# Gate columns as float32 products in four column groups of the array, added by a 0/1 product

## The chip, the cores and the metric

The kernel runs on one core of a Trainium2 chip. The metric is device time in microseconds (us), the median of three runs.

## What is computed

Two transformer blocks on one sequence of 512 tokens of width 1024, all in float32. Block one begins with a root-mean-square norm and one wide projection, whose columns are split into thirteen parts. Three of these parts are very narrow: 8 columns `a_f`, 4 columns `b_i` and 4 columns `b_f`. They are the gates that the change is about.

```python
h = _rms(x, norm_mix_g[l])
z = h @ w_in + b_in
(a_q, a_k, a_v, a_f, b_qk, b_v, b_i, b_f, b_o, c_q, c_f, c_i, c_g) = _split_cols(z)
ca = jnp.cumsum(jax.nn.log_sigmoid(a_f.astype(f32)), axis=1).transpose(0, 2, 1)
ob = _mlstm_chunkwise(_heads(qb, B_HEADS), _heads(kb, B_HEADS), _heads(b_v, B_HEADS),
                      b_i.astype(f32).transpose(0, 2, 1), b_f.astype(f32).transpose(0, 2, 1))
```

## The kernel before, in words

**Products.** A large product is made from three matmuls of type fp32r: each operand is split into a high part (rounded by ScalarE) and a low part (the rest, by VectorE), and high times high, low times high and high times low are added in one bank (lines 1031 to 1033; 1301 to 1305 for the first tile pair). The activations of block one are `act_hi` and `act_lo`, made from `xin` (x transposed, 8 slices of 128 rows by 512 tokens) times the gain `g_mix`; the factor per token, `rsx`, is multiplied in where a tile leaves its bank.

**Weights.** They come in chunks of up to 2048 columns per partition. SyncE loads chunk c into `w_raw[c % 2]` once chunk c - 2 is split; ScalarE makes `w_hi[c % 3]` (line 1574) and VectorE `w_lo[c % 3]` (line 1918). When a chunk is split follows from a plan: chunk c is due after the last tile that reads chunk c - 3, unless the order names it (`w_later`).

**Tiles.** A tile is 128 output channels by 512 tokens in one PSUM bank, `ring0` or `ring1` in turn, or a bank of its own. TensorE says `tile_done`; VectorE drains the tile, and with that frees the ring (`ring_free`). Plain float32 matmuls are used beside these for small steps: `x_rs` (line 1081, ones times the squares, 128x512) and `hg_win` (line 1118), which runs as pairs, one matmul into partitions 0 to 63 and one into 64 to 127.

**Order.** One list of stages, `order`, is written out by hand, and every engine walks through it, each doing its own part of a stage. So a stage's place in the list is its place in every engine's queue. Around the change the list reads:

```python
        stage("w_later", 4)
        stage("hg_begin")
        products(2)
        in_tile("gates", 0, "gates")
        products(1)
        stage("gate_ln")
        ...
        for b in range(NB):
            stage("cb_a", b)
            fill_slot()
```

`hg_begin` and `products(n)` (stages `hg_att`, lines 2103 to 2109) are VectorE work of the HGRN heads; `fill_slot` puts one more `products(1)` and, at every fourth slot, four `hg_win` into the list. `cb_a` (four stages, 12 matmuls each) begins the tiles of `c_i` and `b_v` with chunk `cb0`, and `cb` ends them with chunk `cb1`. The gates are chunk 2: 1024 columns, of which 16 hold weights, and 24 matmuls of 128x512 (8 slices times 3). VectorE drains them into `gz` (line 1962), ScalarE adds the bias and makes the logarithms (stage `gate_ln`).

Of the kernel before, what the change touches and what calls it, by code (L numbers as in the profile page):

```python
# [99 lines left out]
def two_blocks(nc, xt_d, w_in_d, b_in_d, w_gate_d, w_out_d, w_up_d, w_down_d, pos_d, w_in2_d, lam_d, w_uq_d, w_ukv_d,  # L100
               w_pd_d, w_pm_d, w_out2_d, g_fin_d, par_d, con_d, out_d):
    ctx = ExitStack()
    with ctx:
        base = 1152

        def sb(name, shape, dt, kib):

            return nc.alloc_sbuf_tensor_at(name, shape, dt, offset=base + int(round(kib * KIB)))

        def sem(name):  # L110
            return ctx.enter_context(nc.semaphore(name))
# [10 lines left out]
        x_in = [sem(f"x_in{k}") for k in range(KD)]  # L122
        w_in0 = sem("w_in0")

        zeros_ready = sem("zeros_ready")

        x_sq, x_sum, x_ss, x_rs, x_hi, x_lo, x_col, z_in = (
# [7 lines left out]
        hg_a, hg_a_used, hg_q, hg_att_s, hg_kdT_mm, hg_kdT_s = (  # L135
            sem(n) for n in ("hg_a", "hg_a_used", "hg_q", "hg_att_s", "hg_kdT_mm", "hg_kdT_s"))

        hg_kd, hg_cross_mm, hg_sc, hg_u_mm, hg_u_s, hg_scan, hg_rep_mm, hg_dm, hg_in_mm, hg_o_mm, hg_n, hg_done = (
            sem(n) for n in ("hg_kd", "hg_cross_mm", "hg_sc", "hg_u_mm", "hg_u_s", "hg_scan", "hg_rep_mm", "hg_dm", "hg_in_mm", "hg_o_mm", "hg_n", "hg_done"))

        nrm_sq, nrm_mm, nrm_rs, nrm_done, qk_done = (sem(n) for n in ("nrm_sq", "nrm_mm", "nrm_rs", "nrm_done", "qk_done"))

# [60 lines left out]
        kdE = [sb(f"kdE{i}", [P, 2, NC, LC], F32, M + 44 + 4 * i) for i in range(2)]  # L203
        Ab = [sb(f"Ab{i}", [P, 2, T], F32, M + (12, 16, 28, 32, 36, 40)[i]) for i in range(6)]
        kd = sb("kd", [P, 2, NC, LC], F32, M + 20)
        kdT = sb("kdT", [P, 2, NB, P], F32, M + 24)
        qT = sb("qT", [P, 4, T], F32, M + 28)
        kT = sb("kT", [P, 4, T], F32, M + 36)
# [92 lines left out]
        def cc(name, r=slice(0, P)):  # L301
            at, n = CCOL[name]
            return con[r, at:at + n]

        def pc(name, i=0, n=1, r=slice(0, P)):
            return par[r, PCOL[name][0] + i:PCOL[name][0] + i + n]
# [34 lines left out]
        def chunk(name, *areas):  # L341
            parts, at = [], 0
            for sources in areas:
                if not isinstance(sources, list):
                    sources = [sources]
                nk, n = sources[0].shape[1], sum(src.shape[2] for src in sources)
                parts.append((at, nk, n, sources))
                at += nk * n
            assert at <= SLOT
            chunk_of[name] = len(chunks)  # L350
            chunks.append((name, parts, at))
# [24 lines left out]
        def stage(*s):  # L376
            order.append(s)
# [3 lines left out]

        in_chunk("c_f", OFF_CF)
        in_chunk("c_q", OFF_CQ)
        chunk("gates", w_gate_d)
        for q in range(2):
            chunk(f"cb{q}", [k_in[:, 4 * q:4 * q + 4, at:at + 256] for at in (OFF_CI, OFF_BV)])
        for i in range(2):
# [7 lines left out]
        def in_tile(kind, i, of):  # L395
            if (kind, i) in tile_at:
                last_use[chunk_of[of]] = tile_at[kind, i]
            else:
                tile((kind, i), of)
            stage(kind, i)  # L400
# [55 lines left out]
        begin("c_q", 1, KD)  # L456
        for p in range(2):
            in_tile("c_f", p, "c_f")
        in_tile("c_q", 0, "c_q")
        for p in range(2):  # L460
            stage("z", "c_f", p)
# [5 lines left out]
        stage("w_later", 4)  # L467
        stage("hg_begin")
        products(2)
        in_tile("gates", 0, "gates")  # L470
        products(1)
        stage("gate_ln")
        windows = iter(range(LC - 1, -1, -1))
        slots = itertools.count()

        def fill_slot():
            n = next(slots)
            if n % 4 == 3:
                for _ in range(4):
                    stage("hg_win", next(windows))  # L480
            if n < 13:
                products(1)

        for b in range(NB):
            stage("cb_a", b)
            fill_slot()
        for b in range(NB):
            in_tile("cb", b, "cb1")
# [405 lines left out]
        def bank_free(name):  # L894

            return ring_free[tile_at[name] % 2]

        def drains(name):

            return tile_at[name] // 2 + 1  # L900
# [61 lines left out]
        @block.sync  # L962
        def _(sp):
            x_k = xt_d.rearrange("(k p) t -> p k t", p=P)

            def weights_in(c):
                name, parts, n = chunks[c]
                for at, nk, w, sources in parts:
                    dst = raw[c % 2][:, at:at + nk * w].rearrange("p (k n) -> p k n", k=nk)
                    col = 0  # L970
                    for src in sources:
                        sp.dma_start(dst[:, :, col:col + src.shape[2]], src).then_inc(raw_in[c % 2], 16)
                        col += src.shape[2]

            def columns(c, k0, k1):
                return raw[c][:].rearrange("p (k n) -> p k n", k=KD)[:, k0:k1, :], chunks[c][1][0][3][0][:, k0:k1, :]

            for k in range(KD):
                sp.dma_start(xin[:, k, :], x_k[:, k, :]).then_inc(x_in[k], 16)
                sp.dma_start(*columns(0, k, k + 1)).then_inc(w_in0 if k == 0 else x_in[k], 16)  # L980
            sp.dma_start(*columns(1, 0, KD // 2)).then_inc(raw_in[1], 16)
            sp.dma_start(*columns(1, KD // 2, KD)).then_inc(raw_in[0], 16)
            sp.dma_start(con[:, 0:2 * P + 1], con_d[:, 0:2 * P + 1]).then_inc(con_in, 16)
            sp.dma_start(par[:, KD:], par_d[:, KD:]).then_inc(par_in, 16)
            sp.wait_ge(raw_in[0], 16)
            for c, (name, parts, n) in enumerate(chunks):
                if c >= 2:
                    wait_split(sp, c - 2)
                    weights_in(c)
                if c == 3:  # L990
                    sp.dma_start(con[:, 2 * P + 1:], con_d[:, 2 * P + 1:]).then_inc(rest_in, 16)
                    for i, (at, w) in enumerate(((OFF_AV, 512), (OFF_BV, 256), (OFF_CI, 256))):
                        to = (0, 512, 768)[i]
                        sp.dma_start(bias_t[:, to:to + w], b_in_d[at:at + w].partition_broadcast(P)).then_inc(rest_in, 16)
                    sp.dma_start(lamv[:].rearrange("p a b -> p (a b)"), lam_d.partition_broadcast(P)).then_inc(rest_in, 16)
                if name == "wo_b1":

                    sp.wait_ge(tile_done, upto(("yb", 1)))
                    sp.wait_ge(yb_n, 1)
                    for i in range(2):  # L1000
                        sp.dma_start(xT[:, 4 * i:4 * i + 4, :], x_k[:, 4 * i:4 * i + 4, :]).then_inc(x_back_in[i], 16)
                if name == "gate3":

                    sp.dma_start(posI[:], pos_d.partition_broadcast(P)).then_inc(pos_in, 16)

            sp.wait_ge(tile_done, upto(("pm", KD - 1)))
            sp.dma_start(gfin[:], g_fin_d.partition_broadcast(P)).then_inc(gfin_in, 16)
            for b in range(NB):
                for half, made in enumerate((out_act, out_dve)):
                    at = slice(512 * half, 512 * half + 512)  # L1010
                    sp.wait_ge(made, b + 1)
                    sp.dma_start(out_d.rearrange("(b p) d -> p b d", p=P)[:, b, at], xo[:, b, at]).then_inc(out_done, 16)
            sp.wait_ge(out_done, 32 * NB)
# [3 lines left out]
        def _(pe):  # L1017
# [57 lines left out]
            for s in order:  # L1075
                kind = s[0]
                if kind == "x_rs":

                    pe.wait_ge(con_in, 16)
                    pe.wait_ge(x_sum, KD - 1)  # L1080
                    pe.matmul(bank[4][:], cc("ones"), xsq[:, 0, :], start=True, stop=True).then_inc(x_ss, 1)
                elif kind == "gates":
                    channels(s, kind, 0, act)
                elif kind in ("c_g", "b_o"):
                    channels(s, kind, P * s[1], act, begun=begun.get(s, 0))
                elif kind in ("b_qk", "a_q", "a_k"):
# [73 lines left out]
                elif kind == "hg_in":  # L1160
                    p = s[1]
                    pe.wait_ge(hg_dm, 4)
                    for b in range(NB):
                        for hh in range(2):
                            r = slice(64 * hh, 64 * hh + 64)
                            mm = pe.matmul(bank[2 * p + hh][r, b * P:b * P + P], ci[:, b, (2 * p + hh) * HD:(2 * p + hh + 1) * HD],
                                           Dm[2 * p + hh][:, b, :], start=(b == 0), stop=False)
                    mm.then_inc(hg_in_mm, 1)
                elif kind == "hg_o":
                    p = s[1]  # L1170
                    pe.wait_ge(hg_scan, p + 1)
# [380 lines left out]
        def _(act):  # L1552
# [23 lines left out]
            for s in order:  # L1576
# [50 lines left out]
                    act.wait_ge(bank_free(s), drains(s))  # L1627
                    A(bo[:, s[1], :], bo[:, s[1], :], ACT.Sigmoid, bias=pc("b_bo", s[1])).then_inc(z_in, 1)
                elif kind == "gates":
                    act.wait_ge(bank_free(s), drains(s))  # L1630
                    A(gz[:], gz[:], ACT.Identity, bias=pc("b_gate", r=slice(0, 96))).then_inc(z_in, 1)
                elif kind == "gate_ln":

                    act.wait_ge(z_in, z_at["gates", 0])
# [264 lines left out]
        def _(dve):  # L1899
# [21 lines left out]
            for s in order:  # L1921
# [30 lines left out]
                elif kind in ("c_f", "c_q"):  # L1952
# [3 lines left out]
                    dve.wait_ge(x_rs, 1)  # L1956
                    to = cf[:, p] if kind == "c_f" else cq[:, p, :, 0:LC]
                    TT(to, v3(at_ring(s)[:], LC), v3(rsx[:], LC), ALU.mult).then_inc(bank_free(s), 1)
                elif kind == "gates":

                    dve.wait_ge(tile_done, upto(s))
                    TT(gz[:], at_ring(s)[0:96, :], rsx[0:96, :], ALU.mult).then_inc(bank_free(s), 1)
                elif kind in ("b_qk", "c_g", "b_o", "a_q", "a_k"):

                    i = s[1]
# [124 lines left out]
                elif kind == "hg_att":  # L2090
                    j = s[1]
                    n = LC - 1 - j
                    if n >= 6:
                        dve.wait_ge(hg_a_used, n - 5)
                    if n == 2:
                        dve.wait_ge(tile_done, upto(("gates", 0)))
                    q64 = cq[:].rearrange("p h c t -> p (h c) t")
                    f64 = cf[:].rearrange("p h c t -> p (h c) t")
                    k64 = ck[:].rearrange("p h c t -> p (h c) t")
# [533 lines left out]
```

## Time and profile before

| | |
|---|---|
| median of 3 runs | 1093.14 us (1093.06 to 1093.54) |
| span of the profiled execution | 1091.2 us (first to last instruction) |
| median less that span | 1.9 us |
| TensorE busy | 1078.4 us |
| VectorE busy | 713.4 us |
| ScalarE busy | 421.6 us |
| DMA over the span | 95.94 MB |

For the profiled execution only its span is listed. Busy times of TensorE overlap and their ends are modelled, so how long a matmul keeps the array is read from the chain of work, where each piece runs to the start of the next.

### The profile page before, as it was taken

The page shows a single profiled execution, that of the slowest core. Times are in us where ns is not written, and L with a number is a line of the kernel's source. Part 1 is how long each engine was busy: PE and PEld are TensorE (multiplying, and loading weights), DVE is VectorE, ACT ScalarE, POOL GpSimd, SP SyncE. Part 2 cuts the span into 40 slices and gives each one's busy share as a digit, 9 for nine tenths or more (in the row PEclk, how much of TensorE's full clock was granted, in tenths as well). Part 3 has the DMA queues.
Part 4 walks back from the last instruction along what each step waited for, and adds up shares of the span by engine and source line. Part 5 has one row for each costly group of instructions (what it writes and reads, how often), then busy time and mean ns, then how long its engine had stood idle before and what let it go on. Part 6 is the DMA issues. An engine that isn't in the chain of part 4 may idle for free.

```text
span 1091.2 us, 13622 instructions
## 1 busy us (share of the span) xinstructions
PE 1078.4 (99%) x5409; PEld 868.7 (80%) x5411; DVE 713.4 (65%) x1142; ACT 421.6 (39%) x663; POOL 0.2 (0%) x4
## 2 busy tenths in 40 slices
PE   9999999999999999999999999999999999999997
PEld 6877877877878888888888888887776777888886
DVE  6897877868768887754488745654568446364431
ACT  6612555334352323222222234744357443323232
POOL 0000000000000000000000000000000000000000
PEclk9999999999999999999999999999999999999999
DMA  8432121131213223233422134333121222033302
GB/s 256 121 116 78 39 77 41 57 136 39 78 39 126 97 97 106 58 87 101 151 78 87 49 97 154 92 102 116 44 78 39 78 77 78 1 117 115 111 25 77
DMA packets 100240, 95.94 MB, mean 88 GB/s; under 512 B 5953, under 2 KB 91089, under 8 KB 100177
## 3 DMA queue, kind: packets, MB, share of 16 engines
q1 hardware_dynamic: 100000, 95.05, 27.2%
q8 instruction: 43, 0.70, 0.3%
q14 instruction: 21, 0.16, 0.0%
q10 hardware_dynamic: 176, 0.02, 0.0%
HBM read 92.95 MB, written 2.10 MB: 87 GB/s over the span
## 4 chain that ended last, share of the span: by engine, by line
PE 94%; DVE 3%; ACT 1%; issue 1%; DVEq 0%; ACTq 0%
PE ring L1031 23%; PE ring L1033 22%; PE ring L1032 22%; PE bank L1031 3%; PE bank L1033 3%; PE bank L1032 3%; PE bank L1486 1%; PE bank L1281 1%; PE bank L1253 1%; PE bank L1186 1%; PE bank L1266 1%; PE bank L1118 1%; PE bank L1510 1%; PE bank L1459 1%; PE ring L1349 1%
## 5 line engine op out<-in xcount | busy, mean ns | idle before, releaser
L1031 PE MATMUL ring<-act_hi,w_hi 128*128 128x512 f32 (+1 forms) x816 | 323.5, 396 | 0.9 <-DVE xT L2302 0.5
L1033 PE MATMUL ring<-act_hi,w_lo 128*128 128x512 f32 (+1 forms) x816 | 316.7, 388 | 0.0
L1032 PE MATMUL ring<-act_lo,w_hi 128*128 128x512 f32 (+1 forms) x816 | 316.4, 388 | 0.0
L1574 ACT ACTIVATE w_hi<-w_raw 128x2048 fp32r<-128x2048 f32 (+4 forms) x97 | 160.9, 1659 | 248.1 <-PE ring L1033 212.8
L1918 DVE TENSOR_TENSOR w_lo<-w_raw,w_hi 128x2048 fp32r<-128x2048 f32 (+5 forms) x102 | 191.4, 1879 | 4.0 <-ACT w_hi L1574 3.7
L1031 PEld LDWEIGHTS ring<-act_hi,w_hi 128*128 128x128 f32 x816 | 153.3, 188 | 37.4 <-issue 3.9
L1032 PEld LDWEIGHTS ring<-act_lo,w_hi 128*128 128x128 f32 x816 | 153.3, 188 | 31.8 <-issue 1.9
L1033 PEld LDWEIGHTS ring<-act_hi,w_lo 128*128 128x128 f32 x816 | 153.2, 188 | 31.7
L1033 PE MATMUL ring<-hidH,w_lo 128*128 128x512 f32 x176 | 68.5, 389 | 0.0
L1031 PE MATMUL ring<-hidH,w_hi 128*128 128x512 f32 x176 | 68.5, 389 | 0.0
L1032 PE MATMUL ring<-hidL,w_hi 128*128 128x512 f32 x176 | 68.5, 389 | 0.0
L2336 DVE TENSOR_TENSOR zp<-ring,rsn 128x512 f32<-128x512 f32 x44 | 30.3, 689 | 41.6 <-PE ring L1033 37.0
L1911 DVE CUSTOM_DVE_ANT_0 bank<-bank,maskb 128x128 f32<-128x128 f32 (+3 forms) x80 | 37.7, 513 | 28.4 <-PE bank L1513 13.7
L2361 DVE TENSOR_TENSOR xT<-xT,ring 128x512 f32<-128x512 f32 x16 | 11.0, 686 | 58.1 <-PE ring L1033 58.1
L1032 PEld LDWEIGHTS ring<-hidL,w_hi 128*128 128x128 f32 x176 | 33.0, 188 | 6.9
L1031 PEld LDWEIGHTS ring<-hidH,w_hi 128*128 128x128 f32 x176 | 33.0, 188 | 6.8
L1033 PEld LDWEIGHTS ring<-hidH,w_lo 128*128 128x128 f32 x176 | 33.0, 188 | 6.8
L1574 ACT ACTIVATE hidH<-hid 128x512 fp32r<-128x512 f32 x22 | 13.8, 625 | 60.3 <-DVE hid L2349 60.3
L1574 ACT ACTIVATE Pf<-bank,small 128x128 f32<-128x128 f32 (+3 forms) x32 | 16.6, 523 | 31.4 <-DVE small L1911 31.4
L1574 ACT ACTIVATE sqn<-ring 32x512 f32<-32x512 f32 x36 | 21.2, 589 | 12.6 <-PE ring L1033 12.2
L1031 PE MATMUL bank<-w_hi,mH 128*128 128x512 f32 x64 | 25.7, 402 | 0.0
L1031 PE MATMUL bank<-w_hi,act_hi 128*128 128x512 f32 x64 | 25.4, 397 | 0.0
(360 smaller groups left out, 1624.4 us busy)
## 6 DMA issues: line engine op xcount, KB each, us to landing
w_raw<-in_w_in SPq DMA_DIRECT2D x30, 1024.0 KB, 5.1
w_raw<-in_w_up SPq DMA_DIRECT2D x22, 1024.0 KB, 5.0
w_raw<-in_w_out SPq DMA_DIRECT2D x8, 1024.0 KB, 5.0
w_raw<-in_w_down SPq DMA_DIRECT2D x8, 768.0 KB, 4.6
w_raw<-in_w_down SPq DMA_DIRECT2D x8, 640.0 KB, 4.3
w_raw<-in_w_in SPq DMA_DIRECT2D x7, 512.0 KB, 5.8
xin<-in_xt SPq DMA_DIRECT2D x8, 256.0 KB, 4.2
xT<-in_xt SPq DMA_DIRECT2D x2, 1024.0 KB, 6.6
```

The costliest lines, as they stand in the source:

```text
L1031: pe.matmul(out, ah, bh, start=(first and n == 0), stop=False)
L1032: pe.matmul(out, ah, bl, start=False, stop=False)
L1033: mm = pe.matmul(out, al, bh, start=False, stop=(last and n == len(pairs) - 1))
L1118: mm = pe.matmul(v3(bank[0][64 * p:64 * p + 64, :], LC)[:, :, first:], con[:, row:row + 64], v3(Ab[n % 6][:, p, :], LC)[:, :, first:], sta ...
L1186: pe.matmul(nrm_bank(n)[:], cc("blk"), scr[n % 2][:], start=True, stop=True).then_inc(nrm_mm, 1)
L1253: pe.matmul(bank[e][:, 0:n], qT[r, h // 2, qb * P:qb * P + P], kT[r, h // 2, 0:n], start=True, stop=False)
L1266: mm = pe.transpose(bank[2 + u % 2][:, b * P:b * P + P], Pf[u % 4][:, b * P:b * P + P], ident)
L1574: return act.activation(out, src, func, **more)
L1911: return dve.tensor_tensor_reduce(scores[:, 0:n], scores[:, 0:n], maskb[:, T - n:T], -1.0, 3.0e38, ALU.add, ALU.min, least)
L1918: return TT(dst, full, hi.bitcast(F32), ALU.subtract)
L2336: TT(z[:, 2:T + 2], at_ring(s)[:], rsn[:], ALU.mult).then_inc(bank_free(s), 1)
L2361: TT(xT[:, j, :], xT[:, j, :], at_ring(s)[:], ALU.add).then_inc(bank_free(s), 1)
```

## The change

The gates no longer form a chunk of weights. A table `wg` of 352 columns is loaded near the start: 8 blocks of 32 columns (16 of them used), one for each slice of `xin`, and a 0/1 table of 96 columns. VectorE multiplies the 256 weight columns by `g_mix` (stage `gate_w`). Stage `gatep` makes 8 plain float32 matmuls of 32 columns by 512 tokens, straight from `xin`: in two rounds of four, each of the four into another 32 partitions of one bank. VectorE drains the bank times `rsx` into `scr1`. Stage `gates` is now one float32 matmul of the 0/1 table with `scr1`, which adds the four groups and puts the rows where the rest wants them; it stands behind the first `cb_a`. ScalarE adds the bias from the bank.

```diff
@@
+        wg = sb("wg", [P, KD * 32 + 96], F32, M + 24)
@@
         in_chunk("c_f", OFF_CF)
         in_chunk("c_q", OFF_CQ)
-        chunk("gates", w_gate_d)
@@
             in_tile("c_f", p, "c_f")
+        stage("gate_w")
         in_tile("c_q", 0, "c_q")
@@
         stage("hg_begin")
         products(2)
-        in_tile("gates", 0, "gates")
+        tile(("gatep", 0))
+        stage("gatep", 0)
         products(1)
-        stage("gate_ln")
@@
             stage("cb_a", b)
+            if b == 0:
+                stage("gates", 0)
+                stage("gate_ln")
             fill_slot()
@@ sync
             sp.dma_start(par[:, KD:], par_d[:, KD:]).then_inc(par_in, 16)
+            sp.dma_start(wg[:], w_gate_d).then_inc(gate_in, 16)
@@ tensor
+                elif kind == "gatep":
+                    out = open_bank(s)
+                    pe.wait_ge(gate_w, 1)
+                    for r in range(2):
+                        for j in range(4):
+                            at = 32 * (2 * j + r)
+                            mm = pe.matmul(out[32 * j:32 * j + 32, :], wg[:, at:at + 32], xin[:, 2 * j + r, :], start=(r == 0), stop=(r == 1))
+                    mm.then_inc(tile_done, 1)
                 elif kind == "gates":
-                    channels(s, kind, 0, act)
+                    pe.wait_ge(bank_free(("gatep", 0)), drains(("gatep", 0)))
+                    pe.matmul(bank[4][0:96, :], wg[:, KD * 32:], scr[1][:], start=True, stop=True).then_inc(x_ss, 1)
@@ scalar
                 elif kind == "gates":
-                    act.wait_ge(bank_free(s), drains(s))
-                    A(gz[:], gz[:], ACT.Identity, bias=pc("b_gate", r=slice(0, 96))).then_inc(z_in, 1)
+                    act.wait_ge(x_ss, 2)
+                    A(gz[:], bank[4][0:96, :], ACT.Identity, bias=pc("b_gate", r=slice(0, 96))).then_inc(z_in, 1)
@@ vector
-                elif kind == "gates":
+                elif kind == "gate_w":
+                    dve.wait_ge(gate_in, 16)
+                    by_k = wg[:, 0:KD * 32].rearrange("p (k n) -> p k n", k=KD)
+                    TT(by_k, by_k, wide(pc("g_mix", 0, KD), 32), ALU.mult).then_inc(gate_w, 1)
+                elif kind == "gatep":
 
                     dve.wait_ge(tile_done, upto(s))
-                    TT(gz[:], at_ring(s)[0:96, :], rsx[0:96, :], ALU.mult).then_inc(bank_free(s), 1)
+                    TT(scr[1][:], at_ring(s)[:], rsx[:], ALU.mult).then_inc(bank_free(s), 1)
@@
                     n = LC - 1 - j
                     if n >= 6:
                         dve.wait_ge(hg_a_used, n - 5)
-                    if n == 2:
-                        dve.wait_ge(tile_done, upto(("gates", 0)))
```

As chunk 2 is gone, every later chunk has a number less by one: `cb0` is now chunk 2 and is split in its place early in the program (2048 columns where the gates had 1024), `cb1` is chunk 3, and `w_later` 4 now names the chunk of `b_qk0`. Behind the drain of `cb` 0 all queues are as they were, but for buffer numbers.

TensorE, from the last matmul of `c_q` (`con,rsx` is `x_col`, which turns `rsx` into columns), before; the 22 rows left out here are more of the 24 matmuls of the gates, and behind them stands `cb_a` 0:

```order
L1369 MATMUL bank<-con,rsx 128x1 x4
L1031 MATMUL ring<-act_hi,w_hi_53 128x512
...
L1033 MATMUL ring<-act_hi,w_lo_56 128x512
L1031 MATMUL bank<-w_hi_51,act_hi 128x512
L1032 MATMUL bank<-w_lo_54,act_hi 128x512
```

The same place now; the rows left out are the other eleven matmuls of `cb_a` 0, and the last row is the first of `cb_a` 1:

```order
L1384 MATMUL bank<-con,rsx 128x1 x4
L1095 MATMUL ring<-xin,wg 32x512 x8
L1038 MATMUL bank<-w_hi_53,act_hi 128x512
...
L1040 MATMUL bank<-w_hi_53,act_lo 128x512
L1099 MATMUL bank<-scr_106,wg 96x512
L1038 MATMUL bank<-w_hi_53,act_hi 128x512
```

The 24 matmuls are gone; 8 small ones stand in their place, and one more behind 12 matmuls of `cb_a` 0.

VectorE around the drain of the gates, before (`Ab`, `kd`, `cq` are a product stage; the drain is the row with `ring`):

```order
L2109 TENSOR_TENSOR cq<-cq,cf 128x64x2 [waits hg_a,dve_step]
L2103 TENSOR_TENSOR Ab_76<-cq,ck 128x64x2 [waits dve_step]
L2105 TENSOR_TENSOR kd<-cq,ck 128x64
L2109 TENSOR_TENSOR cq<-cq,cf 128x64x3 [waits hg_a,dve_step]
L1962 TENSOR_TENSOR gz<-ring,rsx 96x512 [waits tile_done,dve_step]
L1918 TENSOR_TENSOR w_lo_55<-w_raw_49,w_hi_52 128x2048 [waits w_hi_done]
```

And now:

```order
L2126 TENSOR_TENSOR cq<-cq,cf 128x64x2 [waits hg_a,dve_step]
L2120 TENSOR_TENSOR Ab_76<-cq,ck 128x64x2 [waits dve_step]
L2122 TENSOR_TENSOR kd<-cq,ck 128x64
L2126 TENSOR_TENSOR cq<-cq,cf 128x64x3 [waits hg_a,dve_step]
L1981 TENSOR_TENSOR scr_106<-ring,rsx 128x512 [waits tile_done,dve_step]
L1933 TENSOR_TENSOR w_lo_55<-w_raw_49,w_hi_52 128x2048 [waits w_hi_done]
```

The drain has the same place, behind `hg_begin` and two product stages; what it writes, `scr1`, is what the new matmul of line 1099 reads.

## Rows read from the trace of the kernel before

**Rows 1.** The page: busy time of the engines (us, share, instructions)

```profile
PE 1078.4 (99%) x5409; PEld 868.7 (80%) x5411; DVE 713.4 (65%) x1142; ACT 421.6 (39%) x663; POOL 0.2 (0%) x4
```

**Rows 2.** Waits of TensorE, whole span: us in total, times, longest

```profile
PE bank L1459 <- ACT P L1574: 2.1, 4, 0.8
PE bank L1070 <- DVE zeros L1920: 1.2, 1, 1.2
```

**Rows 3.** The chain that ended last, 28 to 52 us: start, us, what

```profile
29.43 0.79 PE bank L1369 x8
30.22 0.35 PE ring L1031
...
35.83 0.23 PE bank L1031
...
38.55 0.23 PE bank L1031
...
46.71 1.51 PE bank L1118 x16
48.22 0.43 PE bank L1031
```

**Rows 4.** VectorE in order of time around the drain: start, us, what

```profile
34.69 0.55 DVE L2005 TENSOR_SCALAR cf<-cf,small 128x512 f32<-128x512 f32 x1 [1.27 <-ACT cq L1574]
...
41.42 0.69 DVE L1962 TENSOR_TENSOR gz<-ring,rsx 96x512 f32<-96x512 f32 x1
42.03 2.28 DVE L1918 TENSOR_TENSOR w_lo<-w_raw,w_hi 128x2048 fp32r<-128x2048 f32 x1
...
49.17 0.62 DVE L2103 TENSOR_TENSOR Ab<-cq,ck 128x448 f32<-128x448 f32 x1
```

**Rows 5.** The chain over 0 to 140 us: a float32 128x512 matmul

```profile
24.48 0.86 PE bank L1081 x2
```

**Rows 6.** TensorE by line and shape: the matmuls of line 1118 that come first

```profile
L1118 PE MATMUL bank<-Ab,con 128*64 128x512 f32 x8 | 2.1, 605 | 0.0
L1118 PE MATMUL bank<-Ab,con 128*64 128x64 f32 x4 | 0.3, 219 | 0.0
```

**Rows 7.** Line 1118: durations (ns, min/median/max) of its weight loads

```profile
L1118 PEld LDWEIGHTS bank<-Ab,con x64: 132/136/138, 46.6 to 87.8; 128*64 128x64 f32 x64
```

**Rows 8.** The end of the span: last matmul; then busy times, clock (after POOL), DMA

```profile
1084.70 0.39 PE L1033 MATMUL bank<-w_hi,mL 128*128 128x512 f32 x1
...
1088.00:1089.00 1.00, 0.00 (x0) 0.00 (x0) 0.00 (x0) 0.00 (x0) 0.00 (x0) 1.00 0.97 358
1089.00:1090.00 1.00, 0.00 (x0) 0.00 (x0) 0.00 (x0) 0.00 (x0) 0.00 (x0) 0.55 0.46 166
```

**Rows 9.** The chain at the start of the program, 0 to 8.5 us

```profile
1.18 4.88 PE bank L1070 x11
...
6.91 0.37 PE ring L1305
7.28 0.23 PE ring L1301
```

**Rows 10.** ScalarE, VectorE and SyncE's queue in order of time, early part

```profile
19.00 1.05 ACT L1574 ACTIVATE w_hi<-w_raw 128x1024 fp32r<-128x1024 f32 x1
25.38 0.69 ACT L1574 ACTIVATE rsx<-bank,con 128x512 f32<-128x512 f32 x1 [5.32 <-PE bank L1081]
...
23.55 1.22 DVE L1918 TENSOR_TENSOR w_lo<-w_raw,w_hi 128x1024 fp32r<-128x1024 f32 x1
26.83 1.29 DVE L1958 TENSOR_TENSOR cf<-ring,rsx 128x512 f32<-128x512 f32 x2 [1.91 <-ACT rsx L1574]
...
15.50 0.33 SPq L972 DMA_DIRECT2D w_raw<-in_w_gate  x1
```

**Rows 11.** DMA issues of 0 to 30 us: median us to landing

```profile
w_raw<-in_w_in SPq DMA_DIRECT2D x6, 512.0 KB, 6.2
w_raw<-in_w_gate SPq DMA_DIRECT2D x1, 512.0 KB, 3.5
```

More of the change, by code:

```diff
@@ L123, in two_blocks @@
         w_in0 = sem("w_in0")
+        gate_in, gate_w = (sem(n) for n in ("gate_in", "gate_w"))
         zeros_ready = sem("zeros_ready")
@@ L136, in two_blocks @@
             sem(n) for n in ("hg_a", "hg_a_used", "hg_q", "hg_att_s", "hg_kdT_mm", "hg_kdT_s"))
-        hg_kd, hg_cross_mm, hg_sc, hg_u_mm, hg_u_s, hg_scan, hg_rep_mm, hg_dm, hg_in_mm, hg_o_mm, hg_n, hg_done = (
-            sem(n) for n in ("hg_kd", "hg_cross_mm", "hg_sc", "hg_u_mm", "hg_u_s", "hg_scan", "hg_rep_mm", "hg_dm", "hg_in_mm", "hg_o_mm", "hg_n", "hg_done"))
+        hg_kd, hg_cross_mm, hg_sc, hg_u_mm, hg_u_s, hg_scan, hg_dm, hg_o_mm, hg_n, hg_done = (
+            sem(n) for n in ("hg_kd", "hg_cross_mm", "hg_sc", "hg_u_mm", "hg_u_s", "hg_scan", "hg_dm", "hg_o_mm", "hg_n", "hg_done"))
         nrm_sq, nrm_mm, nrm_rs, nrm_done, qk_done = (sem(n) for n in ("nrm_sq", "nrm_mm", "nrm_rs", "nrm_done", "qk_done"))
@@ L1165, in _ @@
                             r = slice(64 * hh, 64 * hh + 64)
-                            mm = pe.matmul(bank[2 * p + hh][r, b * P:b * P + P], ci[:, b, (2 * p + hh) * HD:(2 * p + hh + 1) * HD],
-                                           Dm[2 * p + hh][:, b, :], start=(b == 0), stop=False)
-                    mm.then_inc(hg_in_mm, 1)
+                            pe.matmul(bank[2 * p + hh][r, b * P:b * P + P], ci[:, b, (2 * p + hh) * HD:(2 * p + hh + 1) * HD],
+                                      Dm[2 * p + hh][:, b, :], start=(b == 0), stop=False)
                 elif kind == "hg_o":
@@ L2610 @@
     cols("b_fconv", a["ffn_conv_b"][0])
-    w_gate = _np.zeros((P, KD, P), _np.float32)
-    for row, at, n in ((0, OFF_AF, AH), (32, OFF_BI, BH), (64, OFF_BF, BH)):
-        w_gate[:, :, row:row + n] = w_in[:, at:at + n].reshape(KD, P, n).transpose(1, 0, 2)
+    w_gate = _np.zeros((P, KD * 32 + 96), _np.float32)
+    by_k, pick = w_gate[:, 0:KD * 32].reshape(P, KD, 32), w_gate[:, KD * 32:]
+    for row, col, at, n in ((0, 0, OFF_AF, AH), (32, 8, OFF_BI, BH), (64, 12, OFF_BF, BH)):
+        by_k[:, :, col:col + n] = w_in[:, at:at + n].reshape(KD, P, n).transpose(1, 0, 2)
         par[row:row + n, PCOL["b_gate"][0]] = b_in[at:at + n]
+        for j in range(4):
+            for i in range(n):
+                pick[32 * j + col + i, row + i] = 1.0
     lam = _np.concatenate([a[f"diff_lambda_{v}_2"][0] for v in ("q1", "k1", "q2", "k2")])
```

## The prediction

> **What bounds the kernel now.** I read the busy times first: TensorE is busy for 1078.4 of 1091.2 us [rows 1], so nearly everything it is spared or made to wait comes out at the end. The waits of TensorE come next: the longest single one is the 1.2 us at the start, and the largest sum is 2.1 us over four waits in block two [rows 2]. There is thus hardly any idle time in which a delay of TensorE could be given back. Third, the chain that ended last around the gates, for what each piece costs [rows 3]: a fp32r matmul of 128x512 keeps the array for 0.23 us, and from 30.22 to 48.22 us the chain is TensorE without a break. Fourth, VectorE in order of time: it is behind TensorE here. TensorE ends the gates at 35.83 us [rows 3], yet VectorE drains them only from 41.42 to 42.11 us [rows 4], 5.6 us later, because `hg_begin` and two product stages stand ahead of the drain in its queue. In the old kernel nobody on TensorE waits for that drain soon, so the lateness costs nothing.
>
> **What TensorE is spared.** The 24 matmuls run from 30.22 to 35.83 us: 5.61 us, all on the chain [rows 3].
>
> **What the 8 small matmuls cost.** A float32 matmul of 512 columns keeps the whole array for 0.86 us [rows 5]. None of 32 columns in width is in the trace; the nearest are the pairs of line 1118, which use 64 columns of the array each. Their first group is four pairs with 512, 64, 96 and 128 columns (the first two shapes stand in [rows 6]), 800 per half. At 0.86 us per 512 that is 1.34 us if the halves run at once and 2.69 us if they run in turn. Measured are 1.51 us, and the next full matmul takes 0.43 in place of 0.23 us [rows 3]: 1.71 us in all, so the halves do run at once, plus 0.37 us for going into the narrow form and back. For four at once: 2 x 0.86 + 0.37 = 2.1 us. The bounds: 2.1 us, and 8 x 0.86 + 0.37 = 7.25 us if all run in turn. I take 2.1, from the nearest row.
>
> The trace speaks against a rule here. Four pairs make 16 weight loads of 136 ns, 2.2 us of loads [rows 7], in a group that costs 1.71 us in all, so loads lie beside matmuls of the other half. The Trainium skill (TensorE: Matmul & The Clock Gate, section on the mechanism of row and column tiling) says that a weight load overlaps a running matmul only where the row group differs. Column groups share their rows, and by that rule the eight matmuls would run nearly in turn, 7.25 us in place of 2.1.
>
> **What the 0/1 matmul costs.** 96 wide, 512 long, float32: 0.86 us [rows 5], nothing for a change of form. Without any wait the edit would thus give 5.61 - 2.1 - 0.86 = 2.65 us.
>
> **The wait it adds.** TensorE reaches `gatep` at 30.2 us as before: its ring is free and `gate_w` is done, since VectorE passes there between 28 and 29 us (below). It ends `gatep` at 32.3 and the 12 matmuls of `cb_a` 0 (2.72 us, from 35.83 to 38.55, [rows 3]) at 35.0 us. Then comes the 0/1 matmul, which waits until `gatep` is drained into `scr1`. That drain has kept its place on VectorE, behind the same `hg_begin` and products; it ends at 42.11 us [rows 4] and nothing ahead of it got faster, for the start of `hg_begin` is set by ScalarE (the 1.27 us wait in the row at 34.69). So TensorE stands from 35.0 to 42.15 us: **7.1 us idle**, with all of `cb_a` 1 to 3, `hg_win` and `cb` queued behind. The 0/1 matmul ends at 43.0, and with 0.1 us for the first matmul behind a wait, `cb_a` 1 begins at 43.15 in place of 38.55 us: **+4.6 us**. The number of column groups at work does not matter to this sum, as the drain sets it.
>
> **The clock.** TensorE's granted clock drops when it idles. The only such place in the trace is the end: the last matmul starts at 1084.70 us and is over by 1085.1; the grant is still 1.00 in 1088 to 1089 us and 0.55 on average in 1089 to 1090 [rows 8], so it fell to half (1.2 GHz) near 1089.1, 4.0 us after the last matmul. A gap of 7.1 us is well beyond that. How it rises is seen at the start: from 1.18 to about 7.28 us fourteen matmuls of 512 columns take 0.44 us each on average, then 0.23 [rows 9]. Fourteen at half clock cost 6.10 in place of 14 x 0.23 = 3.2 us: 2.9 us lost. Bounds for the restart: 0 (the grant holds through the gap) and 2.9. I take 2.5, near the upper one, as one row at the start and one at the end are all there is and I do not expect the restart to meet the slowest case: **+2.5 us**.
>
> **What I cost at nothing.** (a) The early split of chunk 2 has 2048 in place of 1024 columns. On ScalarE the old one is over at 20.05 us, and 5.32 us of waiting follow [rows 10]: 0.9 us more fit in. Its load is issued at 15.50 as before and is 1 MB in place of 0.5; with the 6.2 us that the 512 KB loads of this time took [rows 11], it lands by 22.2, is split high by 24.1 and low by 26.4, still ahead of the drain at 26.83 that waits for `rsx` [rows 10]. If it were later, the drain at 41.42 and the end would be later by as much. (b) `gate_w`, 128x256 on VectorE, at most 0.5 us after 28.0 us; it is hidden by the 1.27 us wait at 34.69 [rows 4]. (c) The load of `wg` is 0.18 MB in a queue that has nothing to start between 9.8 and 15.5 us. (d) VectorE and ScalarE lose the gates' own split (1.22 and 1.05 us) and win nothing with it, as neither sets the end. (e) The product stage at 49.17 us [rows 4] is the first that needs a buffer back from `hg_win`. Since `hg_win` begins about 7 us later, VectorE waits there, 4 to 5 us; TensorE next needs VectorE at the second `hg_win`, 48 matmuls (11 us) on, and one split of 2.28 us is gone from between. No wait of TensorE comes of it. (f) The bias and logarithms of the gates on ScalarE come 1 to 2 us later and are read far behind.
>
> **Sum.** 4.6 + 2.5 = +7.1 us: the span goes from 1091.2 to 1098.3, the median, 1.9 us above its span, from 1093.14 to **1100.2 us**. A difference of 0.2% (2.2 us) is about what a measurement can tell from none.
>
> **Rivals.**
>
> *The gap without the clock.* The grant does not fall, or rises at once. For it: the one fall in the trace took 4.0 us, and a restart may come when only a little is left. Against it: 7.1 us is nearly twice as long. It gives 1093.14 + 4.6 = 1097.7 us. Chance 0.12.
>
> *The column groups run in turn.* `gatep` then ends at 37.5, `cb_a` 0 at 40.2, and the gap is only 2.0 us; the start behind it is again at 43.15 us, and in 2.0 us the clock does not fall: it held for 4.0 [rows 8]. It gives 1097.7 us as well, slower for TensorE's work but better for its clock. If they run two at once, `gatep` takes 3.8 us and the gap is 5.4 us: still the forecast. Chance 0.04 for running in turn. The rule of the Trainium skill named above (TensorE: Matmul & The Clock Gate) would lead here.
>
> *The gain arrives.* If VectorE had drained by 35.0 us, TensorE would never wait and the change would give its 2.65 us: 1090.5 us, faster. The point from which it decides is the drain at 41.42 us: it would have to come 7 us earlier, or TensorE would have to find later waits to give the 7 us back, of which there are 12.8 us in all, 6.1 of them behind the last matmul. Nothing in the diff moves the drain. Chance 0.03, and 0.02 for something between that ends within 0.2%.
>
> *A late start.* Load or split of `cb0` end later than in (a), or the restart is slower than the start of the program: 1101 to 1103 us. Chance 0.06.
>
> The forecast keeps 0.73. The range: 1097.4 takes in both cases without a clock loss, 1101.6 the full 2.9 us and another us of late start; what is left out is the gain and the worst late starts. Slower by over 0.2%: 0.95 (0.73 + 0.12 + 0.04 + 0.06); within: 0.02; faster: 0.03.
>
> **What would show it.** In the profile after: a wait of TensorE of about 7 us for VectorE's drain (line 1981) at the 0/1 matmul, from about 35 to 42 us; a granted clock below 1.00 there and for some us after 42; the eight matmuls in about 2 us; a VectorE wait for TensorE's line 1118 near 50 us; the same rows as before, shifted by 7 us, from 60 us on. The prediction is wrong if the drain comes before 38 us, if the clock stays at 1.00, or if the shift at 60 us does not last to the end.

## The result and the profile after

The changed kernel takes 1101.06 us (median of 5 runs, 1100.48 to 1101.24) against 1093.25 us before (5 runs): a ratio of 1.007, 95% interval 1.0059 to 1.008, so 7.8 us slower. The prediction was 1100.2 us, in a range of 1097.4 to 1101.6. The profile was taken of an execution of 1101.13 us, with a span of 1099.3 us (1091.2 before).

First the waits of TensorE, whole span, as in [rows 2]:

```profile
PE bank L1099 <- DVE scr L1981: 7.1, 1, 7.1
PE bank L1474 <- ACT P L1589: 2.1, 4, 0.8
PE bank L1077 <- DVE zeros L1935: 1.2, 1, 1.2
```

The first row is new: the 0/1 matmul stood 7.1 us for the drain. The other two are those of before. TensorE in order of time shows how the eight matmuls went (the last number of a row is how many records it merges; a float32 matmul leaves two):

```profile
30.21 1.93 PE L1095 MATMUL ring<-xin,wg 128*32 128x512 f32 x16
32.07 0.50 PE L1038 MATMUL bank<-w_hi,act_hi 128*128 128x512 f32 x1
```

From start to start they keep the array for 1.86 us, plus 0.2 for the slower first matmul behind them. VectorE's queue at the same place, to be laid beside [rows 4]:

```profile
34.73 0.55 DVE L2024 TENSOR_SCALAR cf<-cf,small 128x512 f32<-128x512 f32 x1 [0.96 <-ACT cq L1589]
...
41.42 0.69 DVE L1981 TENSOR_TENSOR scr<-ring,rsx 128x512 f32<-128x512 f32 x1
42.03 2.28 DVE L1933 TENSOR_TENSOR w_lo<-w_raw,w_hi 128x2048 fp32r<-128x2048 f32 x1
...
55.19 0.62 DVE L2120 TENSOR_TENSOR Ab<-cq,ck 128x448 f32<-128x448 f32 x1 [6.05 <-PE bank L1134]
```

The drain starts at 41.42 us, to the hundredth where it started before, although its tile was ready 9 us earlier. The chain that ended last, from there on, as in [rows 3]:

```profile
42.17 2.02 PE bank L1099 x2
44.19 0.43 PE bank L1038
...
47.60 0.32 PE bank L1040
47.92 0.23 PE bank L1038
...
54.06 1.51 PE bank L1134 x16
```

`cb_a` 1 begins at 44.19 instead of 38.55 us, its matmuls take 0.43 us each until 47.6, and `hg_win` begins at 54.06 instead of 46.71: 7.35 us late. The granted clock, by stretches (the number before the last two; those are DMA share and GB/s):

```profile
35.00:38.00 3.00, 0.10 (x1) 0.00 (x0) 2.54 (x6) 2.01 (x2) 0.00 (x0) 0.90 0.34 118
38.00:39.00 1.00, 0.00 (x0) 0.00 (x0) 0.79 (x3) 0.00 (x0) 0.00 (x0) 0.50 0.00 0
...
47.00:48.00 1.00, 1.00 (x5) 0.82 (x4) 0.93 (x3) 0.97 (x2) 0.00 (x0) 0.67 1.08 384
48.00:49.00 1.00, 1.00 (x6) 0.82 (x5) 0.97 (x3) 0.18 (x1) 0.00 (x0) 1.00 0.92 316
```

The clock stands at 1.00 or at 0.50 (2.4 or 1.2 GHz), so a mean between the two tells when it changed. A mean of 0.90 over 35 to 38 us puts the fall at 37.4, 2.3 us after TensorE went idle (35.1); 0.67 in 47 to 48 puts the rise at 47.7, 5.5 us after TensorE began again. From there to 677 us every matmul is 7.3 to 7.4 us later than before. One more piece is added at the end of block one:

```profile
685.80 1.13 PE L1379 MATMUL bank<-sacc,con 128*128 128x512 f32 x2 [0.41 <-DVE sacc L2327]
...
1092.83 0.39 PE L1040 MATMUL bank<-w_hi,mL 128*128 128x512 f32 x1
```

This matmul (the sum of squares for block two's norm) began at 677.82 before, without a wait; now it waits 0.41 us for VectorE's sum and begins 8.0 us late, 0.6 more than what runs ahead of it. The last matmul starts at 1092.83 against 1084.70 in [rows 8]: 8.1 us late.

### The profile page after: what moved, and what is told of

Same layout as the page of the kernel before. It is cut to its first block, busy times and chain, and to the rows that moved or that the text cites. A ratio compares the mean times of both kernels' runs of the same rounds, so it can differ in the third digit from the quotient of the medians.

```text
span 1099.3 us, 13610 instructions
## 1 busy us (share of the span) xinstructions
PE 1079.4 (98%) x5405; PEld 866.6 (79%) x5405; DVE 712.8 (65%) x1142; ACT 420.8 (38%) x662; POOL 0.2 (0%) x4
## 4 chain that ended last, share of the span: by engine, by line
PE 92%; DVE 4%; ACT 2%; issue 1%; DMA 1%; DVEq 0%; ACTq 0%
PE ring L1038 22%; PE ring L1040 22%; PE ring L1039 22%; PE bank L1038 3%; PE bank L1039 3%; PE bank L1040 3%; PE bank L1501 1%; PE bank L1296 1%; PE bank L1268 1%; DVE w_lo L1933 1%; PE bank L1201 1%; PE bank L1281 1%; PE bank L1134 1%; PE bank L1525 1%; PE bank L1474 1%
## 5 line engine op out<-in xcount | busy, mean ns | idle before, releaser
L1038 PE MATMUL ring<-act_hi,w_hi 128*128 128x512 f32 (+2 forms) x808 | 320.5, 397 | 0.9 <-DVE xT L2319 0.5
L1040 PE MATMUL ring<-act_hi,w_lo 128*128 128x512 f32 (+2 forms) x808 | 313.7, 388 | 0.0
L1039 PE MATMUL ring<-act_lo,w_hi 128*128 128x512 f32 (+2 forms) x808 | 313.4, 388 | 0.0
L1589 ACT ACTIVATE w_hi<-w_raw 128x2048 fp32r<-128x2048 f32 (+5 forms) x96 | 159.8, 1666 | 257.5 <-PE ring L1040 198.8
L1933 DVE TENSOR_TENSOR w_lo<-w_raw,w_hi 128x2048 fp32r<-128x2048 f32 (+4 forms) x101 | 190.3, 1886 | 4.1 <-ACT w_hi L1589 3.8
```

Of the source, the lines that this page charges most:

```text
L1038: pe.matmul(out, ah, bh, start=(first and n == 0), stop=False)
L1039: pe.matmul(out, ah, bl, start=False, stop=False)
L1040: mm = pe.matmul(out, al, bh, start=False, stop=(last and n == len(pairs) - 1))
L1589: return act.activation(out, src, func, **more)
L1933: return TT(dst, full, hi.bitcast(F32), ALU.subtract)
```

## The experiments

All against the kernel before, run beside them on the same chip (1093.22 to 1093.36 us in the three batches). The 1101.06 us of the changed kernel are from another batch; the kernel before agrees within 0.15 us over all four.

**The drain in an earlier place.** Nothing on TensorE moves.

```diff
-        stage("w_later", 4)
-        stage("hg_begin")
-        products(2)
         tile(("gatep", 0))
         stage("gatep", 0)
+        stage("w_later", 4)
+        stage("hg_begin")
+        products(2)
```

> The changed kernel with gatep and its drain ahead of the split of the next chunk, hg_begin and the two product stages; nothing on TensorE is moved. Theory (the loss is VectorE's late drain and what follows from it): VectorE has 0.96 us idle before 34.73 us, so the drain ends near 34.5, the 0/1 matmul waits for nothing, and the saving of 5.6 - 2.0 - 0.9 = 2.7 us comes out: 1090.5 us, granted clock 1.00 throughout. Rival (the float32 matmuls in four column groups, or their switching, cost the time): the time stays near 1101. Rival (the drain put ahead delays hg_begin and hg_win as much): 1093 or more.

Measured: 1091.50 us (11 runs, 1091.09 to 1092.16), ratio 0.9985, interval 0.9976 to 0.9994. Its chain:

```profile
30.35 1.85 PE ring L1095 x16
32.20 0.43 PE bank L1038
...
35.17 0.86 PE bank L1099 x2
36.03 0.23 PE bank L1038
...
44.20 1.51 PE bank L1134 x16
```

No wait, the 0/1 matmul costs its 0.86 us, and `hg_win` begins at 44.20: 2.5 us ahead of the kernel before where the changed kernel was 7.35 us behind. So both rivals fall, and this version beats both kernels. At the end 1.8 us are left of the 2.5 (last part of this section).

**The 0/1 matmul in a later place.**

```diff
             stage("cb_a", b)
-            if b == 0:
+            if b == 3:
                 stage("gates", 0)
                 stage("gate_ln")
```

> The changed kernel with the 0/1 matmul behind cb_a 3 in place of cb_a 0; the drain stays where it is. Theory: TensorE comes to the 0/1 matmul at about 43.1 us, 1 us after the drain; no long wait, no fall of the clock. But hg_win then comes near 44.0 us and its fourth pair needs a VectorE product that ends at 45.7, so about 0.9 us of the 2.7 us is lost there: 1091.4 us. Rival (the eight matmuls cost it): near 1101.

Measured: 1092.14 us (11 runs, 1091.21 to 1092.95), ratio 0.999, interval 0.9981 to 0.9999. With the drain as late as ever, the kernel is 8.9 us below the changed one by asking for it later, against 9.6 us for the early drain; the 0.64 us between the two are in these places of its profile: the first `hg_win` takes 2.1 us in place of 1.5, with one wait of 0.37 us for VectorE's product (none with the early drain; I had expected 0.9 us), and TensorE waits 1.0 against 0.5 us at the end of block one. The spreads of the two overlap.

**The gap filled.** The wait stays, the array does not idle.

```diff
                 elif kind == "gates":
+                    keep_warm(32, bank[0])
                     pe.wait_ge(bank_free(("gatep", 0)), drains(("gatep", 0)))
```

> The changed kernel with 32 bf16 matmuls of zeros, 512 columns each, into a bank not yet in use, ahead of the waiting 0/1 matmul: 32 x 0.216 = 6.9 us of the 7.1 us gap are filled, the wait for the drain stays. Theory (4.6 us of the loss are the gap less the saving, the rest is the half clock after it): the clock stays at 1.00, and the time is 1093.2 + 4.6 = 1097.9 us, or 0.6 us more where the late load at the end of block one comes again. Rival (the clock is not to blame, the rest of the loss lies elsewhere): 1101.

Measured: 1098.04 us (5 runs, 1097.63 to 1098.19), ratio 1.0044, interval 1.0032 to 1.0057. In its trace, TensorE in order of time and then the granted clock:

```profile
34.60 7.08 PE L1077 MATMUL bank<-zeros 128*128 128x512 bf16 x32
41.85 1.10 PE L1100 MATMUL bank<-scr,wg 128*96 128x512 f32 x2 [0.17 <-DVE scr L1982]
```

```profile
42.00:44.00 2.00, 2.00 (x8) 1.28 (x9) 2.00 (x2) 0.98 (x2) 0.00 (x0) 1.00 0.00 0
```

The wait for the drain is worth 4.8 us net of what the edit saves (1098.04 less 1093.27). The other 3.0 us (1101.06 less 1098.04) are not all the clock's. From the start of the 0/1 matmul to `hg_win` the changed kernel needs 11.9 us (42.17 to 54.06), this one 9.3 us (41.85 to 51.16 on its chain): the half clock costs 2.6 us. The rest is the wait of 0.4 us at the end of block one, which this profile does not have.

**Only the wait, in the kernel before.**

```diff
+                    if (kind, b) == ("cb_a", 1):
+                        pe.wait_ge(bank_free(("gates", 0)), drains(("gates", 0)))
```

> The kernel before with one wait added and nothing else: cb_a 1 waits for the drain of the gates. TensorE ends cb_a 0 at 38.55 and the drain ends at 42.15: a gap of 3.6 us. Theory (wait and clock are the whole loss, the new matmuls have no part in it): 1093.3 + 3.6 + 0.1 = 1097.0 us if the clock holds, up to 1100 where it falls. Rival (a wait for VectorE in this place is given back further on): 1093 to 1095.

Measured: 1098.53 us (5 runs, 1098.43 to 1098.98), ratio 1.005, interval 1.0036 to 1.0064. Its chain behind the wait:

```profile
41.92 0.04 issue
41.96 0.50 PE bank L1031
42.47 0.24 PE bank L1032
42.71 0.43 PE bank L1033
...
45.70 0.42 PE bank L1031
46.12 0.23 PE bank L1032
```

The granted clock there:

```profile
42.00:43.00 1.00, 1.00 (x4) 0.81 (x5) 1.00 (x1) 1.00 (x2) 0.00 (x0) 0.79 0.00 0
```

3.6 us of waiting, and then the clock: two matmuls at full speed, eight at half, full again. The fall came at about 42.6 us, when TensorE was already back at work, 4.2 us after it had gone idle (38.4). So 5.3 us are lost without one new matmul, and nothing is given back later.

**One column group in place of four.**

```diff
-                    for r in range(2):
-                        for j in range(4):
-                            at = 32 * (2 * j + r)
-                            mm = pe.matmul(out[32 * j:32 * j + 32, :], wg[:, at:at + 32], xin[:, 2 * j + r, :], start=(r == 0), stop=(r == 1))
+                    for k in range(KD):
+                        mm = pe.matmul(out[0:32, :], wg[:, 32 * k:32 * k + 32], xin[:, k, :], start=(k == 0), stop=(k == KD - 1))
...
-                    pe.matmul(bank[4][0:96, :], wg[:, KD * 32:], scr[1][:], start=True, stop=True).then_inc(x_ss, 1)
+                    pe.matmul(bank[4][0:96, :], wg[0:32, KD * 32:], scr[1][0:32, :], start=True, stop=True).then_inc(x_ss, 1)
```

First in the order of the changed kernel:

> The changed kernel with all eight matmuls into the first 32 partitions, one after the other, and a 0/1 matmul over 32 rows. Theory: they take 8 x 0.86 + 0.37 = 7.25 us in place of 2.0, all of it inside the gap, which shrinks from 7.1 to about 2.0 us; the start behind it stays at 42.2 us. If the clock holds for 2.0 us: 1097.9 us, faster than the changed kernel although TensorE does more. Rival (the clock falls in so short a gap; in the changed kernel it fell 2.3 us after the last matmul): near 1101. Rival (the eight matmuls' own time counts): 1106.

Measured: 1101.38 us (4 runs, 1099.38 to 1102.48). Then in the order of the first experiment, where nothing hides it:

> The kernel of e1 (drain ahead of hg_begin, no long wait) with the eight matmuls into the first 32 partitions and a 0/1 matmul over 32 rows. Here nothing hides their own time. Theory (column groups work at once): the eight take 7.05 us in place of 1.93, and the time is that of e1 plus 5.1: 1096.6 us. Rival (a float32 matmul of 32 columns is quick by itself and the groups give nothing): 1091.5 us as e1.

Measured: 1097.05 us (5 runs, 1096.62 to 1097.57), 5.5 us above four groups. The chain of this one:

```profile
30.45 6.99 PE ring L1093 x16
37.44 0.43 PE bank L1038
```

6.99 us for eight in turn against 1.85 us for eight in four groups: 3.8 times. That is 5.1 of the 5.5 us; the rest is the 0/1 matmul over 32 rows, which with the slower matmul behind it takes 0.4 us more here than the one over 128 rows in the first experiment. In the first of the two runs their own time hides in the gap: with 5 us more work ahead of it, the 0/1 matmul starts at 42.16 us, as it does in the changed kernel (42.17). But my value for the time, 1097.9 with the clock held, was wrong. Its wait and clock:

```profile
PE bank L1097 <- DVE scr L1979: 1.9, 1, 1.9
```

```profile
41.00:42.00 1.00, 0.00 (x0) 0.00 (x0) 0.93 (x3) 0.00 (x0) 0.00 (x0) 1.00 0.00 0
42.00:43.00 1.00, 0.84 (x2) 0.24 (x2) 1.00 (x2) 0.00 (x0) 0.00 (x0) 0.84 0.00 0
...
49.00:50.00 1.00, 1.00 (x5) 0.82 (x4) 0.14 (x1) 0.00 (x0) 0.00 (x0) 0.74 0.00 0
```

Here 1.9 us of waiting let the clock fall, at 42.7 us, half a microsecond after TensorE had resumed, and it stayed low until 49.5. This is one of the two slowest of the four runs (1102.48 us, mean clock 0.995). The other two took 1100.27 and 1099.38 us, with mean clocks of 0.997 and 0.998, so the loss differs from run to run. Another 1.0 us of the profiled run is the wait at the end of block one, taken up below.

**A gap of 2 us behind full-width work.** Is it the length of the gap, or what ran before? The filled gap again, with 24 in place of 32 matmuls of zeros:

> The changed kernel with 24 bf16 matmuls of zeros, 5.2 us, in the gap, so that about 2 us of idleness are left, as many as in the run with one column group, where the clock still fell. Theory (a gap of 2 us is enough for a fall in some executions): the runs spread, between 1097.9 with the clock held and about 1101.5 with it lost. Rival (there it was the seven us of narrow matmuls that let the clock fall, and a gap of 2 us behind full-width work is harmless): all runs near 1098.0 and close together, as with the filled gap.

Measured: 1098.01 us (5 runs, 1097.53 to 1099.09). The wait is again 1.9 us, and the clock stays:

```profile
42.00:43.00 1.00, 1.00 (x3) 0.50 (x4) 1.00 (x1) 0.00 (x0) 0.00 (x0) 1.00 0.00 0
```

So a gap of 1.9 us does not by itself bring the fall. The rival holds for the median and for four of five runs. The fifth, 1.1 us above the median with a mean clock of 0.997 against 0.998 and 0.999, may have lost a little clock; that is not shown, as it has no trace. Nor is it shown which difference decides. In the kernel with one group TensorE ran 7 us of 32-column matmuls and then 2.7 us of full-width ones ahead of the gap, and its 0/1 matmul behind the gap uses 32 rows in place of 128. The narrow matmuls alone do not bring a fall: in the run with one group and the early drain, without a gap, the clock is 1.00 from 28 to 60 us.

**Where the weights lie.** The wait at the end of block one (0.4 us in the changed kernel) follows a load of a weight chunk, which is on the chain there:

```profile
675.42 5.79 DMA w_raw<-in_w_in
681.21 0.02 issue
681.24 0.02 ACT w_hi L1589
...
685.06 0.69 DVE sacc L2327
```

With one chunk less, each later chunk goes to the other raw buffer and another of three split buffers. Two kernels move the buffers back and forth: the first experiment's with the addresses of the kernel before, and the kernel before with those of the changed one.

```diff
-        raw = [sb(f"w_raw{i}", [P, SLOT], F32, 8 * i) for i in range(2)]
+        raw = [sb(f"w_raw{i}", [P, SLOT], F32, 8 * (1 - i)) for i in range(2)]
```

(`whi` and `wlo` are turned as well, by one place in the first kernel and by two, that is back by one, in the second)

> The kernel of e1 with the weight buffers placed so that each later chunk of weights lies at the same address as in the kernel before (one chunk less had moved every chunk to the next buffer). Of e1's 2.5 us ahead of the kernel before, 0.7 us are gone in its profile at the end of block one, where the load of a chunk landed later. Theory (it is where the load is written to): 1090.7 us, and no wait at that place. Rival (it is the landing time of that load as it differs from one execution to the next): 1091.5 us as e1, within the spread of the runs.

> The kernel before with its weight buffers placed as the changed kernel has them, nothing else. Theory (place of the buffer): 1094.0 us. Rival (differs from one execution to the next): 1093.2 us.

Measured: 1091.44 us (11 runs), where the first experiment had 1091.50, and 1093.39 us (11 runs) beside 1093.36 for the kernel before: the addresses make no difference. In the profiles the load took 5.8 to 6.4 us and TensorE waited 0.4 to 1.0 us in six kernels (the changed one, the early drain with either addresses, the late 0/1 matmul, and one column group in both orders); in the others TensorE did not wait, though two of these, the ones with filled gaps, have the same plan of loads as the changed kernel. What makes the load later stays open.

## Why the prediction was right

*The wait.* Right in place and size. It rested on the rows of VectorE's queue before and on the drain keeping its place in the list; both held to 0.1 us. The shift of 4.6 us without the clock is 4.8 in the run with the filled gap, whose chain lies 4.4 to 4.6 us behind.

*The eight matmuls.* I took 2.1 us for four abreast from pairs of two; measured 1.86 + 0.2. The bound for eight in turn, 7.25 us, is 6.99 + 0.2. The rule of the Trainium skill (TensorE: Matmul & The Clock Gate, the mechanism of row and column tiling), that a weight load overlaps a matmul only across row groups, does not hold here: four column groups that share their rows ran 3.8 times as fast as one. The 16 weight loads of the changed kernel's eight matmuls stand in its trace in three bursts, 0.42 us in all, and 1.86 us leave 0.14 beside two matmuls in turn (2 x 0.86), so loads did lie beside running matmuls.

*The clock.* Right that it falls, and right in size: 2.5 us forecast, 2.6 us from the traces of the changed kernel and of the one with the filled gap. The size was in part luck. The bounds were 0 and 2.9 us and the choice between them was a guess, and other gaps cost 1.7 us (3.6 us of waiting) and about 3 us (1.9 us of waiting, one group). The upper bound was read from how long the matmuls at the start take, 0.44 us; the column of the granted clock says 1.00 there, so that half clock is inferred.

*The rival with the groups in turn.* Its price of 1097.7 failed by 3.7 us in the median of the run that tests it, mostly at the step "in 2.0 us the clock does not fall: it held for 4.0". The one fall at the end of the trace does not give a gap that is safe: in that run 1.9 us of waiting sufficed. The wait at the end of block one, 1.0 us in its profile, is the other part.

*Costs put at nothing.* The split of 2048 columns early, `gate_w` and the load of `wg` cost nothing: `hg_begin` starts at 34.73 against 34.69. The landing "by 22.2" is somewhat later than its own terms give (15.50 + 6.2 = 21.7); in the trace after, ScalarE splits that chunk from 20.74 us and VectorE ends at 25.9, ahead of the drain at 26.89. VectorE's wait for `hg_win` came as said, 6.05 us where I had 4 to 5, because the clock delayed `hg_win` as well; nobody waited for VectorE after it. I had no term for the load at the end of block one. In the profile after it is 0.6 of the 1.0 us by which the shift of the last matmul, 8.1 us, exceeds the forecast 7.1; 0.25 more are there already at `hg_win` (7.35). With the early drain that wait is 0.5 of the 0.7 us by which 2.5 shrink to 1.8.

*The rival in which the gain arrives* was out for this kernel, but its arithmetic was sound: 2.65 us, of which 2.5 appear as soon as the drain comes 7 us earlier, and 1.8 at the end.

## What to carry to other kernels

A product taken apart into a part and a sum puts another engine between two matmuls. Before moving it, look up where that engine is at that time: a drain that was late at no cost becomes the bound as soon as the next matmul needs it. With queues in a fixed order the cure is not faster matmuls but place: ask for the drain later, or put it ahead of the long work in the other queue. And count a gap on TensorE with what its clock takes afterwards: here 1.7 us on top of 3.6, and 2.6 on top of the 7.1 us gap.

## What the runs showed of the hardware that I had not expected

The clock can fall after TensorE is back at work: in the kernel with only the wait (gap 3.6 us) at about 42.6 us, 0.6 us after the restart, and in the kernel with one group (gap 1.9 us) 0.5 us after it. From the end of the last matmul to the fall it took 2.3, 4.2 and 2.5 us in these three profiles (changed kernel, wait only, one group) and 4.0 at the end of the kernel before. From the restart to full clock it took 5.5, 4.0 and 7.3 us. So the length of a gap alone does not give its price, and the runs of the kernel with one group spread over 3.1 us, where those of the kernel before spread over 0.9.

Eight float32 matmuls of 32 columns in four column groups took 1.85 us, hardly more than two in turn (2 x 0.86), each group with its own moving operand.
